# Down projections of two blocks: nine of eleven K pairs as seven block products, in two passes over the weights

## The reference

```
f = (silu(h @ w_gate) * (h @ w_up)) @ w_down                   # first block
u = h @ w_up; c = conv_b + sum_j conv_w[j] * up[:, j:j + S]    # second block
gate, val = split(c); f = (silu(gate) * val) @ w_down
```

## Time and profile before

| | before |
|---|---|
| median of 3 runs | 1285.47 us (1285.39 to 1286.33) |
| span of the profiled execution | 1283.5 us |
| PE busy | 1274.3 us, 99% |
| DVE busy | 860.1 us, 67% |
| ACT busy | 682.8 us, 53% |
| POOL busy | 476.5 us, 37% |
| HBM read | 118.32 MB |

### The profile page before, as it was taken

One profiled execution on the slowest core, in us unless ns is written; L12 is line 12 of the kernel. 1 busy time (PEld: TensorE's weight loads), 2 busy tenths in 40 slices (PEclk: granted clock), 3 DMA queues, 4 the chain that ended last, 5 costly groups with the idle time before them and its releaser, 6 DMA issues.

```text
span 1283.5 us, 21963 instructions
## 1 busy us (share of the span) xinstructions
PE 1274.3 (99%) x7792; PEld 1162.0 (91%) x7792; DVE 860.1 (67%) x1597; ACT 682.8 (53%) x1371; POOL 476.5 (37%) x552
## 2 busy tenths in 40 slices
PE   8999999999999999999999999999999999999998
PEld 7999988999999988889999999889898989888887
DVE  6677766799888733364566788467987777533454
ACT  5666745455555522346667788344554545322352
POOL 5655671346565300126777766210213231000000
PEclk9999999999999999999999999999999999999999
DMA  6221213234333342242212323142323232522121
GB/s 205 82 74 59 82 62 120 77 121 130 99 98 98 122 133 98 81 84 74 75 50 67 75 67 116 67 134 70 101 78 115 82 114 66 181 98 98 66 99 66
DMA packets 122752, 121.44 MB, mean 95 GB/s; under 512 B 23309, under 2 KB 109532, under 8 KB 122675
## 3 DMA queue, kind: packets, MB, share of 16 engines
q1 hardware_dynamic: 116352, 112.12, 27.9%
...
...
HBM read 118.32 MB, written 2.10 MB: 94 GB/s over the span
## 4 chain that ended last, share of the span: by engine, by line
PE 98%; DVE 1%; ACT 0%; DMA 0%; issue 0%; POOL 0%; DVEq 0%; ACTq 0%
PE ps L2510 13%; PE ps L2511 13%; PE ps L2512 13%; PE ps L2762 9%; PE ps L2766 9%; PE ps L2764 9%; PE ps L2629 7%; PE ps L2636 6%; PE ps L2631 6%; PE ps L2724 2%; PE ps L2713 2%; PE ps L2712 2%; PE ps L2736 1%; PE ps L2734 1%; PE ps L2522 1%; PE ps L2676 1%
## 5 line engine op out<-in xcount | busy, mean ns | idle before, releaser
L2510 PE MATMUL ps<-h_hi,w_hi 128*128 128x256 f32 (+1 forms) x748 | 238.2, 318 | 0.0
L2511 PE MATMUL ps<-h_lo,w_hi 128*128 128x256 f32 (+1 forms) x748 | 237.4, 317 | 0.0
L2512 PE MATMUL ps<-h_hi,w_lo 128*128 128x256 f32 (+1 forms) x748 | 237.2, 317 | 0.0
L1843 DVE TENSOR_TENSOR w_lo<-w_raw,w_hi 128x512 fp32r<-128x512 f32 x164 | 106.5, 699 | 126.8 <-ACT w_hi L1297 126.4
L1297 ACT ACTIVATE w_hi<-w_raw 128x512 fp32r<-128x512 f32 x164 | 92.0, 620 | 156.8 <-PE ps L2766 133.4
L2762 PE MATMUL ps<-w_hi,st_hi 128*128 128x512 f32 x432 | 169.1, 391 | 0.0
L2766 PE MATMUL ps<-w_hi,st_lo 128*128 128x512 f32 x432 | 168.2, 389 | 0.0
L2764 PE MATMUL ps<-w_lo,st_hi 128*128 128x512 f32 x432 | 168.2, 389 | 0.0
L2629 PE MATMUL ps<-w_hi,h_hi 128*128 128x384 f32 (+2 forms) x512 | 162.6, 328 | 0.0
L2631 PE MATMUL ps<-w_hi,h_lo 128*128 128x384 f32 (+2 forms) x512 | 157.9, 319 | 0.0
L2512 PEld LDWEIGHTS ps<-h_hi,w_lo 128*128 128x128 f32 x748 | 142.5, 191 | 9.6
...
## 6 DMA issues: line engine op xcount, KB each, us to landing
w_raw<-in_w_up_dram SPq DMA_DIRECT2D x25, 1024.0 KB, 5.2
w_raw<-in_w_down_dram SPq DMA_DIRECT2D x22, 1024.0 KB, 4.9
...
w_raw<-in_w_gate_dram SPq DMA_DIRECT2D x11, 1024.0 KB, 5.2
w_raw<-in_w_out_dram SPq DMA_DIRECT2D x8, 1024.0 KB, 5.0
...
w_raw<-in_w_ple_gate_dram SPq DMA_DIRECT2D x4, 1024.0 KB, 5.1
```

What stands on the lines that cost most here:

```text
L1843: dve.tensor_tensor(w_lo[:, slot, q], w_raw[:, slot, q], w_hi[:, slot, q].bitcast(F32), ALU.subtract).then_inc(lo_done, 1)
L2510: pe.matmul(out_, s_hi, m_hi, start=first and n == 0, stop=False, skip_group_check=True)
L2511: pe.matmul(out_, s_hi, m_lo, start=False, stop=False, skip_group_check=True)
L2512: mm = pe.matmul(out_, s_lo, m_hi, start=False, stop=last and n == len(pairs) - 1, skip_group_check=True)
```

## The change

For nine of the eleven pairs the 512 x 256 by 256 x 1024 product is seen as a 2 x 2 product of blocks (two token halves by two features, two features by two column halves) and made from seven block products instead of eight. A block product is two token tiles by three matmuls of 512 columns. The sums of weight blocks are T1 = B12 - B11, T2 = B22 - T1, T4 = T2 - B21 and T3 = B22 - B12; the sums of rows are S1 = A21 + A22, S2 = S1 - A11, S4 = A12 - S2 and S3 = A11 - A21.

Since there are eight banks, this goes in two passes. Steps 0 to 8 (one a pair) make P1 = A11 B11, P5 = S1 T1, P6 = S2 T2 and P4 = A22 T4, each added up over the nine pairs in two banks. Between the passes ScalarE copies P1's banks to SBUF and VectorE adds up what later outputs need, into `hid`, whose rows are free by then. Steps 9 to 17 take the same pairs again, loaded a second time, and make P2 = A12 B21 (into P1's banks), P3 = S4 B22 and P7 = S3 T3. The last two pairs are made as before (`last_rows`), with VectorE's six final additions (`down_fixed`) beside them.

GpSimd makes the weight sums (`down_sums_of`), three to a step of the first pass, one to a step of the second, and there the difference of rows (`row_diff`) too. VectorE makes S1 and S2 in place in `hid` (`rows_summed`) and nearly all low parts. For step 0 of the second layer GpSimd subtracts two low parts (`first_sums_low`). GpSimd's loads of `early_hi` and `early_lo` go between its sums. SyncE loads the nine pairs twice, the second time 768 KB of each in two transfers. Loops over chunks are written out.

```diff
+STRASSEN = 9
+STEPS = 2 * STRASSEN
+PLAIN = MT // RB - STRASSEN
+LEFT, RIGHT = slice(0, 512), slice(512, 1024)
+BANKS = {"P1": (0, 2), "P2": (0, 2), "P6": (1, 3), "P3": (1, 3), "P5": (4, 6), "P7": (4, 6), "P4": (5, 7)}
+W_QUARTER = {"P1": 0, "P5": 1, "P6": 2, "P4": 3, "P2": 0, "P3": 1, "P7": 2}
+A_QUARTER = {"P1": 0, "P4": 1, "P6": 2, "P5": 3, "P2": 0, "P3": 1, "P7": 2}
+W_LOW = {"P1": 1, "P5": 2, "P6": 3, "P4": 3, "P2": 1, "P3": 1, "P7": 2}
+A_LOW = {"P1": 1, "P4": 1, "P5": 2, "P6": 2, "P2": 1, "P3": 2, "P7": 2}
+W_PIECES = {"B11": (0, 1), "T1": (1, 2), "T2": (2, 3), "T4": (3, 4), "T24": (2, 4), "B2": (0, 2), "T3": (2, 3)}
...
+def order_of(d, i):
+    if i == 0:
+        return (("P5", "P4", "P6", "P1"), ("P5", "P1", "P4", "P6"))[d]
+    if i < STRASSEN:
+        return ("P1", "P5", "P6", "P4")
+    return ("P3", "P2", "P7") if i == STEPS - 1 else ("P2", "P3", "P7")
...
+            def down_loads(w, d, c0, slots_free):
+                for i in range(STEPS):
+                    src = rows(w)[i % STRASSEN]
+                    if i < 2:
+                        for sem_, value in slots_free[i]:
+                            sp.wait_ge(sem_, value)
+                    else:
+                        sp.wait_ge(down_sums, weight_sums_at(d, i - 1, 0))
+                        sp.wait_ge(down_lo, weights_lo_at(d, i - 2, 1))
+                    dst, done = down_raw_of(i), down_raw[down_slot(i)]
+                    if i < STRASSEN:
+                        sp.dma_start(dst, src).then_inc(done, 16)
+                    else:
+                        sp.dma_start(dst[:, 1, :], src[:, 1, :]).then_inc(done, 16)
+                        sp.dma_start(dst[:, 0, RIGHT], src[:, 0, RIGHT]).then_inc(done, 16)
+                for n in range(PLAIN):
+                    sp.wait_ge(down_sums, weight_sums_at(d, STEPS - PLAIN + n + 1, 0))
+                    sp.wait_ge(down_lo, weights_lo_at(d, STEPS - PLAIN + n, 1))
+                    load(c0 + n, (c0 + n) % 2, rows(w)[STRASSEN + n], rows=True)
...
+            def down_sums_of(d, i):
+                t, raw = t_sum_w[i % 2], down_raw_of(i)
+                b11, b12, b21, b22 = raw[:, 0, LEFT], raw[:, 0, RIGHT], raw[:, 1, LEFT], raw[:, 1, RIGHT]
+                pool.wait_ge(down_raw[down_slot(i)], raw_at(d, i))
+                if i >= 2:
+                    pool.wait_ge(down_lo, weights_lo_at(d, i - 1, 0))
+                if i < STRASSEN:
+                    pool.tensor_tensor(t[:, 0, :], b12, b11, ALU.subtract).then_inc(down_sums, 1)
+                    pool.wait_ge(down_sums, weight_sums_at(d, i, 1))
+                    pool.tensor_tensor(t[:, 1, :], b22, t[:, 0, :], ALU.subtract).then_inc(down_sums, 1)
+                    pool.wait_ge(down_sums, weight_sums_at(d, i, 2))
+                    pool.tensor_tensor(t[:, 2, :], t[:, 1, :], b21, ALU.subtract).then_inc(down_sums, 1)
+                    return
+                pool.tensor_tensor(t[:, 0, :], b22, b12, ALU.subtract).then_inc(down_sums, 1)
+                pool.wait_ge(row_sums, STRASSEN * d + i - STRASSEN + 1)
+                if i >= STRASSEN + 2:
+                    pool.wait_ge(rows_lo, rows_at(d, i - 2, 2))
+                rows = rows_of_step(i)
+                pool.tensor_tensor(row_diff[:, i % 2, :, :], halves(rows[:, 1, :]), rows[:, 0:1, TOK1].to_broadcast([P, 2, HALF]),
+                                   ALU.subtract).then_inc(row_diffs, 1)
+            def first_sums_low(name, count):
...
+            pool.wait_ge(part_done, parts_done(N_BLOCK - 2, 2))
+            down_sums_of(0, 0)
+            pool.wait_ge(part_done, parts_done(N_BLOCK - 1, 1))
+            for i in range(1, STEPS):
+                down_sums_of(0, i)
+                if 3 <= i < 3 + EARLY_PARTS:
+                    part, src = sources[i - 3]
+                    if i == 3:
+                        pool.wait_ge(hid_done, MT)
+                        pool.wait_ge(down_part, step_end(0, 0))
+                    pool.dma_start(early_hi[:, :, part], src).then_inc(early_high, 16)
+                if 12 <= i < 12 + EARLY_PARTS:
+                    part, src = sources[i - 12]
+                    if i == 12:
+                        pool.wait_ge(early_negated, 2)
+                    pool.dma_start(early_lo[:, :, part], src, accum_op=ALU.add).then_inc(early_low, 16)
...
+            def down_high(d, i, name):
+                if name in ("B11", "B2"):
+                    act.wait_ge(down_raw[down_slot(i)], raw_at(d, i))
+                else:
+                    act.wait_ge(down_sums, weight_sums_at(d, i, {"T1": 1, "T2": 2, "T4": 3, "T3": 1}[name]))
+                if i >= 2:
+                    act.wait_ge(down_part, quarters_free(d, i, W_QUARTER, range(*W_PIECES[name])))
+                act.activation(down_piece(w_hi, i, name), down_source(i, name), ACT.Copy).then_inc(down_hi, 1)
...
+            def first_copied(d):
+                act.wait_ge(down_part, part_at(d, STRASSEN - 1, "P1"))
+                for a in range(2):
+                    act.activation(first_copy[:, a, :], bank_of("P1", a), ACT.Copy).then_inc(down_copied, 1)
...
+            def down_low(d, i, name):
+                dve.wait_ge(down_hi, weights_hi_at(d, i, {"B11": 1, "T1": 2, "T24": 4, "B2": 1, "T3": 2}[name]))
+                dve.tensor_tensor(down_piece(w_lo, i, name), down_source(i, name), down_piece(w_hi, i, name).bitcast(F32),
+                                  ALU.subtract).then_inc(down_lo, 1)
+            def rows_low(d, i, k):
+                first, end = ((0, 2), (2, 4))[k] if i < STRASSEN else ((0, 1), (1, 3))[k]
+                if k == 0:
+                    src = diagonal_rows(i) if i < STRASSEN else rows_of_step(i)[:, 1:2, TOK1]
+                else:
+                    src = halves(rows_of_step(i)[:, 0, :]) if i < STRASSEN else row_diff[:, i % 2, :, :]
+                dve.wait_ge(rows_hi, rows_at(d, i, k + 1))
+                dve.tensor_tensor(row_quarters(st_lo, i, first, end), src, row_quarters(st_hi, i, first, end).bitcast(F32),
+                                  ALU.subtract).then_inc(rows_lo, 1)
...
+            def rows_summed(d, i):
+                early, late = rows_of_step(i)[:, 0, TOK1], rows_of_step(i)[:, 0, TOK2]
+                link(dve.tensor_tensor(late, late, rows_of_step(i)[:, 1, TOK2], ALU.add))
+                dve.tensor_tensor(early, late, early, ALU.subtract).then_inc(row_sums, 1)
...
+            def down_steps(d, start):
+                for i in range(start, STRASSEN):
+                    down_low(d, i, "B11")
+                    rows_low(d, i, 0)
+                    rows_summed(d, i)
+                    down_low(d, i, "T1")
+                    rows_low(d, i, 1)
+                    down_low(d, i, "T24")
+                for i in range(STRASSEN, STEPS):
+                    down_low(d, i, "B2")
+                    if i == STRASSEN + 1:
+                        dve.wait_ge(down_part, part_at(d, STRASSEN - 1, "P6"))
+                        dve.wait_ge(down_copied, 2 * d + 2)
+                        for a in range(2):
+                            dve.tensor_tensor(first_two[:, a, :], bank_of("P6", a), first_copy[:, a, :], ALU.add)\
+                                .then_inc(down_summed, 1)
+                        for a in range(2):
+                            dve.wait_ge(down_summed, 4 * d + 1 + a)
+                            dve.tensor_tensor(kept(0)[:, a], halves(bank_of("P5", a)), halves(first_two[:, a, :]), ALU.add)\
+                                .then_inc(down_summed, 1)
+                    rows_low(d, i, 0)
+                    down_low(d, i, "T3")
+                    rows_low(d, i, 1)
+                    if i == STRASSEN + 2:
+                        dve.wait_ge(down_part, part_at(d, STRASSEN - 1, "P4"))
+                        for a in range(2):
+                            dve.tensor_tensor(kept(1)[:, a], halves(first_two[:, a, :]), halves(bank_of("P4", a)), ALU.subtract)
...
+            def down_part_of(d, i, name):
+                pe.wait_ge(rows_lo, rows_at(d, i, A_LOW[name]))
+                if (d, i) == (1, 0) and W_LOW[name] == 3:
+                    pe.wait_ge(first_sums_lo, 1)
+                else:
+                    pe.wait_ge(down_lo, weights_lo_at(d, i, W_LOW[name]))
+                at_, a = 512 * W_QUARTER[name], HALF * A_QUARTER[name]
+                hi, lo = (w[:, down_slot(i), at_:at_ + 512] for w in (w_hi, w_lo))
+                high, low = (st[:, i % 2, :, :].rearrange("p k n -> p (k n)") for st in (st_hi, st_lo))
+                fresh = i == (STRASSEN if name in ("P3", "P7") else 0) and name != "P2"
+                for n, bank in enumerate(BANKS[name]):
+                    tok = slice(a + P * n, a + P * n + P)
+                    pe.matmul(ps[:, bank, :], high[:, tok], hi, start=fresh, stop=False, skip_group_check=True)
+                    pe.matmul(ps[:, bank, :], high[:, tok], lo, start=False, stop=False, skip_group_check=True)
```

(53 more changed lines are left out.)

384 lines of the change are left out of this document (215 added, 169 removed).

## The result

| | before | after |
|---|---|---|
| median | 1285.49 us (4 runs) | 1316.14 us (4 runs, 1314.54 to 1317.08) |
| span of the profiled execution | 1283.5 us | 1313.4 us |
| PE busy | 1274.3 us, 99% | 1267.6 us, 97% |
| DVE busy | 860.1 us, 67% | 1019.8 us, 78% |
| POOL busy | 476.5 us, 37% | 620.1 us, 47% |

The account below looks back on a forecast made before the run. TensorE's matmuls bound the old kernel; with the change, VectorE and GpSimd taking turns would. Layer 1 +12.1 and layer 2 +18.6 make +30.7 us: 1283.5 becomes 1314.2, and the median, 2.0 above, 1316 us; range 1294 to 1332.

Parts of the forecast that it names:

- matmuls saved, if nothing else held: Down layers: 474 matmuls in place of 528, worth 12.2 us a layer, 24.5 us in all.
- first-pass step: Down layers, steps of the first pass: VectorE's 4.20 us plus three GpSimd sums, 7.7 us against TensorE's 5.44.
- second-pass step: Down layers, steps of the second pass: VectorE's 2.67 us plus GpSimd's 2.3, 5.0 us against TensorE's 4.08.
- Exclusion: Down layers: a GpSimd sum and a VectorE instruction with two SBUF inputs take turns, VectorE ending 0.55 us behind.
- `row_diff`: Second pass: GpSimd's row difference with a broadcast input excludes VectorE like a full sum, 1.15 us in turn.
- The lower end: Range's lower end, 1295 us: `row_diff` excludes nobody, so 18 x 1.15 = 20.7 us would be off.
- Loads at nothing: Down layers' weight loads: 1 MB lands in 4.9 us, each has over 9 us, so no cost.
- Start of layer 1: First down layer: low parts of step 1 end at 457.4, from where the later steps are counted.
- Change of passes: Between the passes: six additions from PSUM, 3.6 us, of which 0.9 beside GpSimd, counted as 2.7.
- Second layer: Second down layer: VectorE's step 1 takes 10.3 us, then the same 98.1; end at 1240.4, +18.6 us.
- Rival, no exclusion: 1263: Down layers: GpSimd and VectorE don't get in each other's way, TensorE stays the bound; 1263 us, chance 0.07.
- Rival, TensorE's clock falls: Down layers: pauses throttle TensorE to half rate; 1434 us throughout, 1340 to 1400 in part; chance 0.05.

Follow-up runs that it names:

- e3_writes: Changed kernel with each GpSimd sum and row difference of the down layers replaced by two fills that read no SBUF; output differs; 1263.97 us, ratio 0.9828.
- e4_nodiff: Changed kernel with only `row_diff` cut to two columns from step 11 on, weight sums whole; output differs; 1307.62 us, ratio 1.0168.
- e1_vector: Changed kernel with GpSimd's down-layer sums and row differences moved to VectorE from step 3 (layer 1) and step 2 (layer 2); 1281.48 us, ratio 0.9968.
- e8_lighter: e1_vector with the third weight sum of each first-pass step that VectorE makes cut to one column; output differs; 1274.74 us, ratio 0.9912.

## Why the prediction was right

The mechanism is the one that was forecast. The time, 1316 against 1316.14, lies closer than its terms do, and that is luck: the span came 0.8 us below the 1314.2 of the sum and the median 2.7 us above that span instead of 2.0 (the spans of the four runs go from 1312.1 to 1314.8). Term by term:

| step of the prediction | predicted | measured |
|---|---|---|
| matmuls saved, if nothing else held | -24.5 us | -21.2 (`e3_writes`, span 1262.3 against 1283.5; 1.5 of the difference lie between the layers) |
| first-pass step | 7.7 us | 7.68 |
| second-pass step | 5.0 us | 4.87 |
| last low rows of layer 1 | 555.5 | 554.17 + 0.68 = 554.85 |
| first matmul behind layer 1 | 583.1 | 582.98 (+11.95 on 571.03) |
| VectorE's steps 9 to 16 and the additions, layer 1 | 40.0 + 2.7 = 42.7 us | 552.10 - 511.30 = 40.80 |
| between the layers | nothing | 13.44 - 11.95 = +1.5 |
| share of layer 2 | +18.6 us | 29.9 - 13.44 = +16.5 |
| sum | +30.7 us | 1313.4 - 1283.5 = +29.9 |

- **Exclusion.** The pairs of the earlier trace rows carried over: 0.55 us behind GpSimd's end for 512 columns, as in the gate stage. The rule of the Trainium skill, "SBUF — State Buffer", section "SBUF: two separate sides", which has this exclusion only against a GpSimd instruction that reads SBUF, is borne out on both its sides: with sums that read SBUF the instruction takes 1.78 us, with fills that only write it takes 0.69.
- **The price in turn.** Step by count is 4.20 + 3 x 1.15 = 7.65, measured 7.68. From the experiments: three sums cost 7.68 - 4.20 = 3.48 us, 1.16 each.
- **`row_diff`.** Taken to exclude like a sum. It does, by the 8.5 us that `e4_nodiff` gave back. The Trainium skill, "SBUF — State Buffer", section "Who interferes with whom", makes no exception for a broadcast, and the 8.5 us agree with it. The lower end, worked out as 20.7 us from 18 turns of 1.15, was too far even for the other case: TensorE's own step stops the gain at 4.08 us, so that 18 x 0.92 = 16.6 us, from the 5.0 of the sum, were the most.
- **Loads at nothing.** Right as to the sum. But they are not early in the second pass: among the waits of 446 to 585 us GpSimd waits seven times for them, 8.8 us in all.

```profile
POOL t_sum_w L1322 <- DMA w_raw<-in_w_down_dram: 8.8, 7, 1.8
```

What hid this is VectorE's full schedule (32.41 of 34 us), and with that cover gone, in `e4_nodiff`, a load showed. The prediction's cover of over 9 us was right only for the slow steps that it forecast. The issues of `early_lo`, up to 3 us for the upper end, took GpSimd 1.27 to 1.34 us each and lengthened no step: one at 536.35 lies within the step of 4.87 us above.
- **Start of layer 1.** VectorE began step 2 at 458.48, not at 457.4: two low parts of step 1 met sums (1.77 us at 453.84 and 1.43 us at 455.87), and the forecast had them at their own length. These 1.1 us too few, and 0.5 too few behind the last low rows (28.1 us where 27.6 were counted), hide that the second pass was counted 1.9 too long.
- **Change of passes.** The additions were counted as 2.7 us of VectorE's and cost less. Of the 40.80 us in the table eight steps of 4.88 are 39.0, so that the additions and a wait of 0.51 us took 1.8. They have an input in PSUM, as L2290 in the earlier trace rows, and don't wait for GpSimd: two of them take 1.27 us together from 517.31 on, within a sum that lasts from 516.76 to 518.51. That TensorE stands still for them was not said. Its timeline:

```profile
518.64 0.50 PE L3070 MATMUL ps<-w_hi,st_hi 128*128 128x512 f32 x1 [2.59 <-DVE first_two L2373]
```

- **Between the layers.** The sum has nothing here, and 1.5 us stand here. TensorE waits at two places where it doesn't in the kernel before, 0.54 us at 852.89 for a `w_lo` (L2045) and here:

```profile
590.12 1.09 PE L2786 MATMUL ps<-ident,h_tok 128*128 128x128 f32 x8 [0.60 <-DVE h_tok L2077]
```

VectorE begins the last product of `hid` at 1117.08, 13.44 us behind the 1103.64 of the earlier trace rows, where the first matmul behind layer 1 was 11.95 us late. `e1_vector` and `e3_writes` lose the same 1.5 us between these two points (from 4.45 us ahead to 2.91, from 10.67 to 9.17), so GpSimd's sums in the down layers are not the cause. What is was not traced.
- **Second layer.** It was counted 2.1 us too dear. VectorE's step 1 took 1127.82 - 1118.31 = 9.5 us where 10.3 was predicted, since one of GpSimd's six sums was already made; steps 9 to 16 with the additions took 1221.74 - 1180.61 = 41.1 where 42.7 was. Against it stands what the sum made before the layer cost there, where the prediction had put nothing: `hid`'s last product waited for it.

```profile
1117.08 1.20 DVE L2568 TENSOR_TENSOR hid<-act_gate,act_val 128x512 f32<-128x512 f32 x1
```

It takes 1.20 us where it took 0.69, and ends at 1118.28. GpSimd's weight sum that began at 1116.43 ended at 1117.72, and VectorE's product of 512 columns 0.56 us behind that.
- **Rival, no exclusion: 1263.** Wrong for the change, and what `e3_writes` gave with the exclusion removed: 1263.97.
- **Rival, TensorE's clock falls.** It does fall, and costs these steps nothing. Two steps of the first pass side by side:

```profile
480.40:488.06 7.66, 5.78 (x24) 4.43 (x24) 7.53 (x8) 3.21 (x7) 5.29 (x4) 1.00 0.63 170
488.10:495.76 7.66, 7.33 (x24) 5.60 (x24) 7.53 (x8) 3.23 (x7) 4.54 (x3) 0.78 0.49 139
```

Both hold 24 matmuls in 7.66 us, the one at a granted clock of 1.00, the other at 0.78 after steps in which TensorE paused for some 2 us. At 1.2 GHz for part of the step it is busy 7.33 of 7.66 us and still done in time: the slack that VectorE leaves takes it up. The Trainium skill, "TensorE: Matmul & The Clock Gate", section "What's actually happening", describes a release that is lost when the array idles; this trace agrees, by its 0.94 from 465 to 526 us against 1.00 in the earlier trace rows. In `e1_vector`, where most pauses are shorter, the granted clock stayed at 1.00. Behind the change of passes the clock is low too: from 520.00 to 522.57 matmuls start 0.43 us apart. TensorE then doesn't wait before 537.60, and VectorE waits once, 0.51 us at 521.82; how much of this is the clock's was not tested.

So the forecast was made by the right mechanism at the right price, and the sizes that were off (too much for the second passes, 1.9 and 1.6 us, and 0.8 for step 1 of layer 2; too little at the start of layer 1, 1.1, behind it, 0.5, between the layers, 1.5, and at `hid` in layer 2, 0.5) nearly cancel. The sharper test was of the repair: the expectation for `e1_vector` was 9 us too good. Its direction followed from the exclusion; its size would have needed the same sum of VectorE's own instructions, 4.20 + 3 x 0.60 = 6.00 us, held against 5.44 through both layers with the changes of passes on top.

The best version that computes everything is `e1_vector`, 0.3% faster than before. Of the 17.5 us that part it from 1264, VectorE's load in the first pass accounts for 9 by count (13 steps at 6.14 instead of 5.44), and `e8_lighter` took 6.7 of them back; the rest was not divided up. A version with evenly spread load, such as plain pairs between the steps of the first pass, was not tried.
